# First attention of a two-block float32 model: projections and softmax steps in one stage, two heads a step

## The chip, the cores and the metric

The kernel runs on one core of a Trainium2 chip. The metric is the device time of one execution in microseconds; the median of several runs is compared. The engines are TensorE (PE, with its weight loads as PEld), VectorE (DVE), ScalarE (ACT), GpSimd (POOL) and SyncE (SP), which here only issues the weights' DMAs.

## The reference, cut to what matters

Two blocks of two layers run one after the other on 512 tokens of width 1024: attention, gated FFNs, a state-space layer, a convolution module, a differential attention, memory cross-attentions. The change touches only the first layer's attention: 8 heads over the whole past with a bias table (A), and 8 query heads on 2 key heads with a band of 128 past tokens and a sink (B).

```python
qa, ka, va, qb, kb, vb = jnp.split(h @ w_in, cuts, axis=-1)      # 18 blocks of 128 columns
qa, ka = rmsnorm(heads(qa, 8), q_norm_a), rmsnorm(heads(ka, 8), k_norm_a)     # over 64, per head
oa = band_attention(qa, ka, heads(va, 8), 8, relpos_table[:, idx], None)
qb, kb = rmsnorm(heads(qb, 8), q_norm_b), rmsnorm(heads(kb, 2), k_norm_b)
ob = band_attention(qb, kb, heads(vb, 2), 2, -slopes * abs(rel_b), sinks)
return concatenate([oa, ob], -1) @ w_out
# band_attention, per chunk of 64 queries:
sc = einsum(q, k) * 0.125 + bias                 # masked to the band
m = max(sc, sink); e = exp(sc - m)
p = e / (sum(e) + exp(sink - m));  out = p @ v
```

## The kernel before, in words

Every projection is a sum of three fp32r products: weights and activations are split into an upper and a lower part. SyncE loads slabs of 512 KB into 4 slots. ScalarE makes the upper part of a slab (`half`, L1840), GpSimd the lower one (`split_stream`, L503), three slabs ahead of TensorE. `gemm` (L545) runs 8 k-steps of three matmuls for each chunk of 128 output channels (L563 to L565) into one of four PSUM banks.

The first attention (`attn`, on TensorE L663, VectorE L1692, ScalarE L2210) has two phases with nothing interleaved.

The first computes 18 chunks: four of queries A, four of keys A, four of queries B, one of keys B, then five of values. VectorE multiplies a chunk by the row norm (L1710), ScalarE squares it (L2238), TensorE sums the squares over each head with a matmul by `head_ones` (L675), ScalarE takes the root (L2227), VectorE the reciprocal (L1717) and multiplies (L1720). Value chunks are transposed on TensorE (L588) and copied by ScalarE (L2221). All go to `qk` and `v_tok`.

The second (`attention`, TensorE L591, VectorE L1201, ScalarE L1867) works 64 units: one head and one tile of 128 queries each, heads A first (32 units with 128 to 512 keys), then heads B (32 units with 128 or 256 keys). Score, bias and mask are matmuls into one bank (L612): the table's bias is a F32 matmul of a reversing matrix `flip` with `rel`, the band's bias and the masks are bf16. VectorE takes the maximum (L1216) and negates it (L1218, or L1221 and L1223 with the sink). ScalarE takes the exponential with its row sum (L1886). VectorE takes the reciprocal (L1232) and scales the row of probabilities (L1235). TensorE transposes it (L625), three units later, ScalarE copies it (L1898), and TensorE multiplies with the values (L639), four units later: stationary 64 value columns, moving 128 queries, so the result comes out as channels by tokens, two heads in the halves of a bank. When a pair of heads is complete, ScalarE writes its upper part `oh` (L1905), VectorE the lower part `ol` (L1247). The output projection then reads them, chunk k behind `a_ol`.

The table is written to DRAM by ScalarE's queue (L2214) and read back in skewed rows by the same queue (`load_rel`, L2208). Each engine runs its instructions in the order written; semaphores hold it until the other engine has done its part.

The diff stage (`diff`, L702, L1267, L1920) near the end of the kernel works two maps of a head side by side (score L782) with projection k-steps between them (L720 to L722).

## Time and profile before

| | us |
|---|---|
| median of 3 runs | 3296.01 (3279.82 to 3302.17) |
| the profiled execution | 3287.4 |
| its span | 3285.5 |
| PE busy | 3129.9 (95%) |
| PEld busy | 2408.3 (73%) |
| DVE busy | 1550.0 (47%) |
| ACT busy | 1269.6 (39%) |
| POOL busy | 1178.6 (36%) |
| mean granted PE clock | 0.974 |

Busy time is the union of an engine's instructions; matmuls overlap, so a busy PE is not PE at its peak. The clock is a share of 2.4 GHz. A view of stretches gives, for each window of the span, the busy time of every engine with its instructions, the clock, the share of the DMA engines and GB/s. A timeline gives start, duration, engine, line, operation and tiles, and in brackets how long the engine was idle before and what ended it.

### The profile page before, as it was taken

What the parts mean: (1) busy time and instruction counts of PE and PEld (TensorE: products, weight loads), DVE (VectorE), ACT (ScalarE), POOL (GpSimd) and SP (SyncE); (2) the same over time, 40 slices, a digit from 0 to 9 for tenths busy, and PEclk for the clock granted to TensorE, in tenths of its full rate; (3) what the DMA queues carried; (4) which work ended last, traced back from release to release, by engine and by line L of the source; (5) the groups of instructions that cost most, each with busy time, mean ns of one, the idle gap of its engine ahead of it and who ended that gap; (6) DMA issues with size and microseconds to landing.
All of it is one profiled execution on the core that took longest, in us unless ns stands there. A gap on an engine that the chain in (4) does not pass through costs nothing.

```text
span 3285.5 us, 40113 instructions
## 1 busy us (share of the span) xinstructions
PE 3129.9 (95%) x13790; PEld 2408.3 (73%) x13790; DVE 1550.0 (47%) x2245; ACT 1269.6 (39%) x1974; POOL 1178.6 (36%) x495
## 2 busy tenths in 40 slices
PE   7999999998998899999998998999989999899998
PEld 5655888886675578888855777888867787788886
DVE  6445555327625744553268633332247763333322
ACT  3234444323334534443322433443233343344432
POOL 3300444443343034444432532444432254144443
PEclk9988999999999899999999999999999999999999
DMA  3200323332220022323311321332322132133332
GB/s 134 83 17 8 96 90 95 97 101 77 83 90 14 1 69 92 95 91 101 98 52 52 115 85 47 94 93 92 103 82 64 59 110 87 42 91 94 96 96 89
DMA packets 73290, 260.51 MB, mean 79 GB/s; under 512 B 8528, under 2 KB 8792, under 8 KB 72928
## 3 DMA queue, kind: packets, MB, share of 16 engines
q1 hardware_dynamic: 68400, 249.07, 24.7%
q10 hardware_dynamic: 4784, 10.05, 0.9%
q8 instruction: 64, 1.05, 0.1%
q14 instruction: 42, 0.34, 0.0%
HBM read 256.97 MB, written 2.12 MB: 79 GB/s over the span
## 4 chain that ended last, share of the span: by engine, by line
PE 43%; issue 36%; POOL 14%; DVE 5%; ACT 1%; POOLq 0%; ACTq 0%; DMA 0%; DVEq 0%
POOL w_lo L503 14%; PE bank L563 11%; PE bank L564 11%; PE bank L565 11%; PE bank L954 2%; DVE bank L1630 2%; PE bank L1081 1%; PE bank L1084 1%; PE bank L639 0%; PE bank L902 0%; PE bank L1098 0%; PE bank L904 0%; PE bank L903 0%; DVE c_u L1616 0%; PE bank L675 0%
## 5 line engine op out<-in xcount | busy, mean ns | idle before, releaser
L503 POOL TENSOR_TENSOR w_lo<-w_raw,w_hi 128x1024 fp32r<-128x1024 f32 x475 | 1145.9, 2414 | 1975.0 <-ACT w_hi L1840 1975.0
L563 PE MATMUL bank<-xh,w_hi 128*128 128x512 f32 x2008 | 811.1, 404 | 37.8 <-DVE xl L1153 15.1
L564 PE MATMUL bank<-xl,w_hi 128*128 128x512 f32 x2008 | 800.5, 399 | 0.0
L565 PE MATMUL bank<-xh,w_lo 128*128 128x512 f32 x2008 | 799.9, 398 | 0.0
L1840 ACT ACTIVATE w_hi<-w_raw 128x1024 fp32r<-128x1024 f32 x475 | 500.9, 1056 | 661.1 <-DMA w_raw<-w_glu_out 156.2
L563 PEld LDWEIGHTS bank<-xh,w_hi 128*128 128x128 f32 x2008 | 381.1, 190 | 145.3 <-issue 24.7
L564 PEld LDWEIGHTS bank<-xl,w_hi 128*128 128x128 f32 x2008 | 381.2, 190 | 95.0 <-issue 4.3
L565 PEld LDWEIGHTS bank<-xh,w_lo 128*128 128x128 f32 x2008 | 381.0, 190 | 93.1
L1186 DVE TENSOR_TENSOR xt<-bank,xt 128x512 f32 x72 | 49.8, 692 | 502.1 <-PE bank L565 502.1
L565 PE MATMUL bank<-hh,w_lo 128*128 128x512 f32 x704 | 279.1, 396 | 0.0
L563 PE MATMUL bank<-hh,w_hi 128*128 128x512 f32 x704 | 279.1, 396 | 0.0
L564 PE MATMUL bank<-hl,w_hi 128*128 128x512 f32 x704 | 279.1, 396 | 0.0
L1758 DVE TENSOR_TENSOR f_u<-bank,rstd 128x512 f32<-128x512 f32 x88 | 60.8, 691 | 275.4 <-PE bank L565 275.4
L1761 DVE TENSOR_TENSOR f_h<-f_y,f_u 128x512 f32<-128x512 f32 x88 | 154.0, 1750 | 7.2 <-ACT f_y L2264 0.3
L2269 ACT ACTIVATE hh<-f_h 128x512 f32 x88 | 55.6, 632 | 260.6 <-DVE f_h L1761 260.6
L564 PEld LDWEIGHTS bank<-hl,w_hi 128*128 128x128 f32 x704 | 132.6, 188 | 32.3
L563 PEld LDWEIGHTS bank<-hh,w_hi 128*128 128x128 f32 x704 | 132.6, 188 | 32.3
L565 PEld LDWEIGHTS bank<-hh,w_lo 128*128 128x128 f32 x704 | 132.6, 188 | 32.3
L1630 DVE SCALAR_TENSOR_TENSOR bank<-c_u,cols,bank 128x512 f32<-128x512 f32 x184 | 125.4, 747 | 44.1 <-PE bank L954 43.5
L1160 DVE TENSOR_TENSOR acc<-acc,sq 128x512 f32<-128x512 f32 x88 | 101.3, 1151 | 70.3 <-ACT sq L1831 70.3
L563 PE MATMUL bank<-oh,w_hi 128*128 128x512 f32 x320 | 128.0, 400 | 3.0 <-DVE ol L1680 2.4
L565 PE MATMUL bank<-oh,w_lo 128*128 128x512 f32 x320 | 126.8, 396 | 0.0
(309 smaller groups left out, 4410.7 us busy)
## 6 DMA issues: line engine op xcount, KB each, us to landing
w_raw<-w_ffn_in SPq DMA_DIRECT2D x88, 512.0 KB, 3.5
w_raw<-w_glu_in SPq DMA_DIRECT2D x88, 512.0 KB, 3.5
w_raw<-w_ffn_out SPq DMA_DIRECT2D x48, 512.0 KB, 3.5
w_raw<-w_glu_out SPq DMA_DIRECT2D x48, 512.0 KB, 3.5
w_raw<-w_ssm_in SPq DMA_DIRECT2D x41, 512.0 KB, 3.5
w_raw<-w_pw SPq DMA_DIRECT2D x24, 512.0 KB, 3.5
w_raw<-w_diff_in SPq DMA_DIRECT2D x24, 512.0 KB, 3.5
w_raw<-w_attn_in SPq DMA_DIRECT2D x18, 512.0 KB, 3.5
```

What stands on the lines that cost most here:

```text
L503: pool.tensor_tensor(w_lo[:, slot, :], w_raw[:, slot, :], w_hi[:, slot, :].bitcast(F32), ALU.subtract).then_inc(w_split, 1)
L563: pe.matmul(b, wh, hi[:, k, 0:n], start=(k == 0), stop=False)
L564: pe.matmul(b, wh, lo[:, k, 0:n], start=False, stop=False)
L565: mm = pe.matmul(b, wl, hi[:, k, 0:n], start=False, stop=last)
L954: mm = pe.matmul(conv_bank(p)[:], c_diag[:, p % 2, n, :], c_u[:, p % 3, n:n + S], start=(n == 0), stop=(n == CPE - 1))
L1160: dve.tensor_tensor(acc[:], acc[:], sq[:, j % 2, :], ALU.add).then_inc(x_acc, 1)
L1186: dve.tensor_tensor(row(xt, c), b[:], row(xt, c), ALU.add).then_inc(bank_free, 1)
L1630: ins = dve.scalar_tensor_tensor(conv_bank(p)[:], c_u[:, p % 3, k:k + S], col("dw_w", CONVW * p + k), conv_bank(p)[:], ALU.mult, ALU.add)
L1758: dve.tensor_tensor(f_u[:], bu[:], rstd[:], ALU.mult).then_inc(bank_free, 1)
L1761: dve.tensor_tensor(f_h[:], f_y[:], f_u[:], ALU.mult).then_inc(f_prod, 1)
L1840: act.activation(w_hi[:, slot, :], w_raw[:, slot, :], ACT.Copy).then_inc(w_half, 1)
L2269: act.activation(row(hh, p), f_h[:], ACT.Copy)\
```

## The change

The two phases become one loop of 32 steps (m), and a step is two heads and one tile of queries. The first four pairs are the banded heads B, the last four are heads A; the weight columns, norm gains, sinks and rows of the output weights are reordered for it. 34 k-steps of projections come first; then each step feeds three portions (x = 3m, 3m+1, 3m+2) of 1.5 k-steps on average, until all 144 are done. A chunk's eviction, its square, its sum over heads, root and reciprocal stand at fixed x (`attn_at`). Chunks use two banks, scores of a step two (four in turn), outputs and their transposes one, sums and value transposes one.

Both heads' scores are issued one behind the other, from partitions 0 to 63 and 64 to 127. The reversing matrix and the table are fp32r; the table is split in an upper and a lower part, two matmuls in place of one. Probabilities are not scaled; the transposed probabilities are now the stationary side and 64 value columns the moving one, so the result is tokens by channels; ScalarE scales it by the reciprocal of the sum while it copies it (`weighed`), and TensorE transposes the pair's 128x128 (`turn_out`). `oh` and `ol` are written per step. Square, sum and root use one buffer each, and root and reciprocal are taken in PSUM. Both table parts go to DRAM by ScalarE's queue and are read back by GpSimd's queue: the first two pairs' ahead of its split of slab 3, the rest behind the last slab of the input projection.

```diff
...
+        BM = 8 * NT
+        NB4 = 4 * NT
+        def is_rel(m):
+            return m >= NB4
+        def keys_of(m):
+            t = m % NT
+            if is_rel(m):
+                return 0, P * (t + 1)
+            return (0, P) if t == 0 else (P * (t - 1), 2 * P)
+        def attn_fed(x):
+            return min(18 * KD, 34 + 9 * (x + 1) // 6) if x >= 0 else 34
+        def attn_at(c, extra):
+            x = 0
+            while attn_fed(x) < min(KD * (c + 1) + extra, 18 * KD):
+                x += 1
+            return x + (1 if KD * (c + 1) + extra > 18 * KD else 0)
...
+        def step_bank(m, half):
+            return bank[2 + 2 * (m % 2) + half]
+        VALUES = (1, 8, 11, 14, 17)
+        NORMED = [c for c in range(18) if c not in VALUES]
...
+            def load_rel(pairs):
+                pool.wait_ge(rel_out, 32)
+                for pair in pairs:
+                    if pair >= 2:
+                        pool.wait_ge(b_score, 2 * (NB4 + NT * (pair - 1)))
+                    for h in (2 * pair, 2 * pair + 1):
+                        pool.dma_start(rel_h[:, h % 4, :], bass.AP(rel_dram_h, h * 767, [[1, P], [1, 640]]))\
+                            .then_inc(rel_buf[h % 4], 16)
+                        pool.dma_start(rel_l[:, h % 4, :], bass.AP(rel_dram_l, h * 767, [[1, P], [1, 640]]))\
+                            .then_inc(rel_buf[h % 4], 16)
...
+                def finish(c):
+                    if c:
+                        if c - 1 in VALUES:
+                            pe.wait_ge(v_ready, 2 + VALUES.index(c - 1) + 1)
+                        else:
+                            pe.wait_ge(q_ready, NORMED.index(c - 1) + 1)
+                    if c in VALUES:
+                        pe.wait_ge(bank_free, BANKS + st.chunk0 + c + 1)
+                        for t in range(NT):
+                            mm = pe.transpose(bank[7][:, t * P:(t + 1) * P], sq[:, 1, t * P:(t + 1) * P], ident[:])
+                        mm.then_inc(v_turned, 1)
                         return
-                    pe.wait_ge(q_sq, c + 1)
-                    if not isinstance(c, int) or c >= 2:
-                        pe.wait_ge(q_root, c - 1)
-                    pe.matmul(bank[5 + j % 2][:], head_ones[:], sq[:, j % 2, :], start=True, stop=True)\
-                        .then_inc(q_sum, 1)
-                def after(c, j):
-                    first_sum(c, j)
-                    if isinstance(c, int) and c == 0:
-                        pe.wait_ge(cst_ready, 4)
-                    lagged(fin, 17)(c, j)
-                gemm(st, xh, xl, S, x_ready(KD * nrm[0]), after, peel=4, tail=6)
-                keep_clock(8)
-                pe.wait_ge(q_ready, 13)
-                pe.wait_ge(flip_done, 2)
-                pe.wait_ge(v_ready, 2 + 5)
+                    pe.wait_ge(q_sq, NORMED.index(c) + 1)
+                    pe.matmul(bank[7][:], head_ones[:], sq[:, 0, :], start=True, stop=True).then_inc(q_sum, 1)
+                def score(m):
+                    pair, t = m // NT, m % NT
+                    k0, nk = keys_of(m)
+                    if t == 0:
+                        pe.wait_ge(q_ready, 5 + 2 * (pair - 3) if is_rel(m) else 2 + pair)
+                    if m >= 2:
+                        pe.wait_ge(b_copied, 2 * (m - 1))
+                    for half in range(2):
+                        lo, hi = 64 * half, 64 * half + 64
+                        q = b_q[lo:hi, (4 + pair - 4) % 6 if is_rel(m) else pair, t * P:(t + 1) * P]
+                        k = b_k[lo:hi, (pair - 4) % 3 if is_rel(m) else 3, k0:k0 + nk]
+                        pe.matmul(step_bank(m, half)[:, 0:nk], q, k, start=True, stop=False, skip_group_check=True)
+                    for half in range(2):
+                        b = step_bank(m, half)
+                        if is_rel(m):
+                            h = 2 * (pair - 4) + half
+                            if t == 0:
+                                pe.wait_ge(rel_buf[h % 4], 32 * (h // 4 + 1))
+                            first = 512 - P * t
+                            pe.matmul(b[:, 0:nk], flip_r[:], rel_h[:, h % 4, first:first + nk], start=False, stop=False,
+                                      skip_group_check=True)
+                            pe.matmul(b[:, 0:nk], flip_r[:], rel_l[:, h % 4, first:first + nk], start=False, stop=False,
+                                      skip_group_check=True)
+                            pe.matmul(b[:, nk - P:nk], ident_b[:], masks_b[:, 0, :], start=False, stop=True,
+                                      skip_group_check=True).then_inc(b_score, 1)
+                        else:
+                            pe.matmul(b[:, 0:nk], ident_b[:], alibi_b[:, 4 * half + pair, 256 - nk:256], start=False, stop=True,
+                                      skip_group_check=True).then_inc(b_score, 1)
...
+                def outputs(m):
+                    pair, t = m // NT, m % NT
+                    k0, nk = keys_of(m)
+                    if t == 0:
+                        pe.wait_ge(v_ready, 2 + 1 + max(pair - 3, 0))
+                    if m:
+                        pe.wait_ge(b_ol, m)
+                    vs = (pair - 4) % 3 if is_rel(m) else 3
+                    for half in range(2):
+                        u = 2 * m + half
+                        pe.wait_ge(b_copied, u + 1)
+                        o = 64 * half
+                        for kt in range(nk // P):
+                            v0 = k0 + kt * P + 64 * half
+                            mm = pe.matmul(bank[6][:, o:o + 64], b_pt[:, u % 4, kt * P:(kt + 1) * P], b_v[:, vs, v0:v0 + 64],
+                                           start=(kt == 0), stop=(kt == nk // P - 1), skip_group_check=True)
+                    mm.then_inc(b_pv, 1)
+                def turn_out(m):
+                    pe.wait_ge(b_otok, m + 1)
+                    pe.transpose(bank[6][:, P:2 * P], b_tok[:, m % 2, :], ident[:]).then_inc(b_ot, 1)
+                feed(KD)
+                norm_sum()
+                pe.wait_ge(cst_ready, 4)
+                feed(KD)
+                finish(0)
+                feed(KD)
+                finish(1)
+                feed(4)
+                finish(2)
+                feed(6)
...
+                for m in range(BM + 2):
+                    if m < BM:
+                        score(m)
+                    for f in range(3):
+                        x = 3 * m + f
+                        feed(attn_fed(x) - attn_fed(x - 1))
+                        for c in range(3, 18):
+                            if attn_at(c, 3) == x:
+                                finish(c)
+                        if f == 0 and 2 <= m <= BM + 1:
+                            outputs(m - 2)
+                        if f == 1 and 1 <= m <= BM:
+                            turn(m - 1)
+                        if f == 1 and 2 <= m <= BM + 1:
+                            turn_out(m - 2)
                 vt[0] = 5
-                attention(*UNITS["attn"])
-                gemm(ST["attn_out"], oh, ol, S, lambda k: pe.wait_ge(a_ol, k + 1))
+                pe.wait_ge(bank_free, BANKS + wo.chunk0)
+                gemm(wo, oh, ol, S, lambda k: pe.wait_ge(b_ol, NT * (k + 1)))
             vt, au, at, ag = [0], [0], [0], [0]
...
-                    dve.wait_ge(q_rec, c + 1)
-                    dst = row(qk, c)
-                    dve.scalar_tensor_tensor(dst, dst, col("g_qk", c),
-                                             rt, ALU.mult, ALU.mult).then_inc(q_ready, 1)
...
+                def peak(m):
+                    _, nk = keys_of(m)
+                    cs = slice(2 * m, 2 * m + 2)
+                    for half in range(2):
+                        u = 2 * m + half
+                        dve.wait_ge(b_score, u + 1)
+                        top = dve.reduce_max(b_stat[:, 0, u:u + 1], step_bank(m, half)[:, 0:nk], AX_X)
+                        if half:
+                            step(top)
+                    if is_rel(m):
+                        dve.tensor_scalar(b_stat[:, 1, cs], b_stat[:, 0, cs], -0.125, None, ALU.mult).then_inc(b_max, 1)
+                        return
+                    sink = sink_c[:, 2 * (m // NT):2 * (m // NT) + 2]
+                    step(dve.scalar_tensor_tensor(b_stat[:, 0, cs], b_stat[:, 0, cs], 0.125, sink, ALU.mult, ALU.max))
+                    step(dve.tensor_scalar(b_stat[:, 1, cs], b_stat[:, 0, cs], -1.0, None, ALU.mult))
+                    dve.tensor_tensor(b_stat[:, 5, cs], sink, b_stat[:, 1, cs], ALU.add).then_inc(b_max, 1)
+                def weigh(m):
+                    cs = slice(2 * m, 2 * m + 2)
+                    dve.wait_ge(b_exp, 2 * m + 2)
+                    if not is_rel(m):
+                        dve.wait_ge(b_sink, m + 1)
+                        step(dve.tensor_tensor(b_stat[:, 2, cs], b_stat[:, 2, cs], b_stat[:, 3, cs], ALU.add))
+                    dve.reciprocal(b_stat[:, 4, cs], b_stat[:, 2, cs]).then_inc(b_rec, 1)
+                def low(m):
+                    ch, t = m // NT, m % NT
+                    dve.wait_ge(b_oh, m + 1)
+                    dve.tensor_tensor(ol[:, ch, t * P:(t + 1) * P], bank[6][:, P:2 * P],
+                                      oh[:, ch, t * P:(t + 1) * P].bitcast(F32), ALU.subtract).then_inc(b_ol, 1)
...
+                for m in range(BM + 2):
+                    if m < BM:
+                        peak(m)
+                    for f in range(3):
+                        x = 3 * m + f
+                        for c in range(3, 18):
+                            if attn_at(c, 3) == x - 1:
+                                finish(c)
+                        for c in range(4, 18):
+                            if attn_at(c, 0) == x:
+                                evict(c)
+                        if f == 0 and 1 <= m <= BM:
+                            weigh(m - 1)
+                    if 2 <= m <= BM + 1:
+                        low(m - 2)
                 vt[0] += 5
-                dve.wait_ge(q_ready, 13)
-                attention(*UNITS["attn"])
                 residual(ST["attn_out"], new_x(nxt[s]))
...
+                def powers(m):
+                    _, nk = keys_of(m)
+                    act.wait_ge(b_max, m + 1)
+                    for half in range(2):
+                        u = 2 * m + half
+                        if m >= 2:
+                            act.wait_ge(b_turn, u - 3)
+                        act.activation(b_prob[:, u % 4, 0:nk], step_bank(m, half)[:, 0:nk], ACT.Exp,
+                                       bias=b_stat[:, 1, u:u + 1], scale=0.125, accum_out=b_stat[:, 2, u:u + 1])\
+                            .then_inc(b_exp, 1)
+                    if not is_rel(m):
+                        cs = slice(2 * m, 2 * m + 2)
+                        act.activation(b_stat[:, 3, cs], b_stat[:, 5, cs], ACT.Exp).then_inc(b_sink, 1)
+                def copied(m):
+                    _, nk = keys_of(m)
+                    for half in range(2):
+                        u = 2 * m + half
+                        act.wait_ge(b_turn, u + 1)
+                        if m >= 2:
+                            act.wait_ge(b_pv, m - 1)
+                        act.activation(b_pt[:, u % 4, 0:nk], step_bank(m, half)[:, 0:nk], ACT.Copy).then_inc(b_copied, 1)
...
+                def weighed(m):
+                    act.wait_ge(b_pv, m + 1)
+                    act.wait_ge(b_rec, m + 1)
+                    if m >= 2:
+                        act.wait_ge(b_ot, m - 1)
+                    for half in range(2):
+                        u, o = 2 * m + half, 64 * half
+                        cp = act.activation(b_tok[:, m % 2, 64 * half:64 * half + 64], bank[6][:, o:o + 64], ACT.Copy,
+                                            scale=b_stat[:, 4, u:u + 1])
+                    cp.then_inc(b_otok, 1)
...
+                for m in range(BM + 2):
+                    if m < BM:
+                        powers(m)
+                    for f in range(3):
+                        x = 3 * m + f
+                        for c in range(3, 18):
+                            if attn_at(c, 3) == x:
+                                finish(c)
+                        for c in range(4, 18):
+                            if attn_at(c, 0) == x:
+                                square(c)
+                        while turned[0] < 18 + LEAD and attn_fed(x) >= min(KD * (turned[0] - LEAD) + 6, 18 * KD):
+                            next_slab()
+                        if f == 0 and 2 <= m <= BM + 1:
+                            weighed(m - 2)
+                        if f == 1 and 1 <= m <= BM:
+                            copied(m - 1)
+                    if 2 <= m <= BM + 1:
+                        upper(m - 2)
                 vt[0] += 5
-                act.wait_ge(rel_out, 16)
-                act.wait_ge(sink_in, 16)
-                for h in range(4):
-                    load_rel(h, None)
-                attention(*UNITS["attn"])
...
```

## Rows read from the trace of the kernel before

**Rows 1.** Busy time in stretches: window, length, engines (instructions), PEclk, DMA share, GB/s
```profile
13.00:154.00 141.00, 126.88 (x487) 93.85 (x488) 85.32 (x66) 47.22 (x65) 46.01 (x20) 0.95 0.26 86
154.00:245.00 91.00, 87.11 (x374) 48.46 (x372) 36.02 (x128) 31.27 (x95) 2.22 (x1) 0.87 0.11 33
245.00:317.00 72.00, 66.23 (x301) 38.33 (x300) 45.97 (x201) 36.62 (x140) 0.00 (x0) 0.81 0.00 1
294.00:310.00 16.00, 16.00 (x51) 8.74 (x50) 8.16 (x34) 6.09 (x24) 0.00 (x0) 0.50 0.00 0
2460.00:2670.00 210.00, 209.87 (x1163) 157.92 (x1163) 161.22 (x364) 83.57 (x201) 65.79 (x27) 1.00 0.21 66
```

**Rows 2.** Timeline of PE: the first matmul of the output projection
```profile
315.62 0.50 PE L563 MATMUL bank<-oh,w_hi 128*128 128x512 f32 x1
```

**Rows 3.** Timeline of PE in the projections: sum over heads, two neighbouring matmuls
```profile
38.02 1.02 PE L675 MATMUL bank<-sq,head_ones 128*128 128x512 f32 x2
...
44.02 0.40 PE L564 MATMUL bank<-xl,w_hi 128*128 128x512 f32 x1
44.26 0.39 PE L565 MATMUL bank<-xh,w_lo 128*128 128x512 f32 x1
```

**Rows 4.** Timeline of PE, table units, 512 keys, from one head to the next
```profile
231.86 1.12 PE L612 MATMUL bank<-qk 64*128 64x512 f32 x2
232.92 1.12 PE L612 MATMUL bank<-rel,flip 128*128 128x512 f32 x2
...
233.94 0.28 PE L625 MATMUL bank<-ident,a_prob_t 128*128 128x128 f32 x1
234.14 1.09 PE L639 MATMUL bank<-a_pt_t,v_tok 128*64 128x128 f32 x8
235.16 0.48 PE L612 MATMUL bank<-qk 64*128 64x128 f32 x2
...
241.85 1.12 PE L612 MATMUL bank<-qk 64*128 64x512 f32 x2
```

**Rows 5.** Timeline of PE, fp32r matmuls of 256 columns
```profile
1795.80 0.28 PE L902 MATMUL bank<-m_hi,w_hi 128*128 128x256 f32 x1
1795.92 0.28 PE L903 MATMUL bank<-m_lo,w_hi 128*128 128x256 f32 x1
```

**Rows 6.** Timeline of PE in diff, scores of two maps side by side
```profile
2585.97 1.13 PE L782 MATMUL bank<-d_k,d_q 64*128 64x512 f32 x4
```

**Rows 7.** Timeline of all engines, one banded unit: maximum, sink, exponential
```profile
284.57 0.41 DVE L1216 TENSOR_REDUCE a_stat<-bank 128x1 f32<-128x256 f32 x1
...
285.46 0.29 ACT L1885 ACTIVATE a_stat<-sink_c,a_stat 128x1 f32<-128x1 f32 x1 [1.53 <-DVE a_stat L1223]
...
285.66 0.46 ACT L1886 ACTIVATE a_prob_t<-bank,a_stat 128x256 f32<-128x256 f32 x1
```

**Rows 8.** Groups by line, 0 to 420 us: count, busy us, mean ns, idle before
```profile
L1717 DVE RECIPROCAL a_prob_t<-a_prob_t 128x512 f32<-128x512 f32 x13 | 43.6, 3351 | 8.2 <-ACT a_prob_t L2227 8.2
...
L1720 DVE SCALAR_TENSOR_TENSOR qk<-qk,cols,a_prob_t 128x512 f32 (+1 forms) x13 | 9.8, 751 | 1.4 <-DVE a_prob_t L1717 1.2
```

**Rows 9.** Timeline of ACT in the state scan: table loads around a root
```profile
1064.68 1.28 ACT L2117 ACT_TABLE_LOAD   x1
...
1066.68 1.28 ACT L2092 ACT_TABLE_LOAD   x1
```

**Rows 10.** A line's durations (min/median/max ns) in diff; a split's group (page)
```profile
L1350 DVE TENSOR_TENSOR d_q<-d_q,acc x8: 691/2742/2744, 2459.4 to 2640.1; 128x512 f32<-128x512 f32 x8
...
L503 POOL TENSOR_TENSOR w_lo<-w_raw,w_hi 128x1024 fp32r<-128x1024 f32 x475 | 1145.9, 2414 | 1975.0 <-ACT w_hi L1840 1975.0
```

**Rows 11.** Timeline of DVE: the first projection chunk leaves PSUM
```profile
33.85 0.69 DVE L1710 TENSOR_TENSOR qk<-bank,rstd 128x512 f32<-128x512 f32 x1
```

**Rows 12.** The line that reads the table: issue ns, landing us (min/median/max)
```profile
L2208 ACTq DMA_DIRECT2D rel<-rel_table x8: 326/334/654, 153.3 to 205.1; - x8
...
DMA to landing us min/median/max: 3.1/4.4/6.3
```

## What the change does to the time: the prediction

> **What bounds the kernel now.** Over the span TensorE is nearly always busy, so a saving must come out of its own time or out of stretches in which it waits. I cut the first attention out of the trace with the view of busy time in stretches [rows 1]. It has three parts with three limits. From 13 to 154 us the 18 projection chunks run; VectorE is busy 85 us of 141 and ScalarE 47, beside TensorE. From 154 to 245 us run the 32 units with a position table, TensorE busy 87 of 91 us. From 245 to 317 us run the 32 banded units; each is small, and TensorE waits in turn for VectorE and ScalarE. The granted clock is 0.81 there, and 0.50 (1.2 GHz) from 294 to 310 us, where the row still calls TensorE fully busy. The output projection begins at 315.62 us [rows 2]; that is the mark which the change can move. The last row of [rows 1] is the attention near the end of the kernel (function diff): 32 steps of two heads with projection matmuls fed between them, 210 us, TensorE busy 209.87, clock 1.00. The change gives that shape to the first attention, so it is my yardstick.
>
> **Prices on TensorE.** At full clock projection matmuls start 0.24 us apart (44.02, 44.26; over a chunk 0.234), and a sum over a head's square, two instructions in F32, takes 1.02 us with its latency, 0.92 in the stream [rows 3]. A table unit at t=3 takes [rows 4]: scores 1.06 us (231.86 to 232.92), table bias in F32 with the bf16 mask 1.02, one transpose 0.20, four outputs 1.02 and thus 0.25 each with the wait. The F32R matmul of 256 columns starts every 0.12 us [rows 5]. Two heads side by side in diff take 1.13 us for four score instructions of 512 columns [rows 6], no more than one head's two: they run together, in two halves of the array.
>
> **The change, part by part.**
> - *Scores.* Per step of two heads 0.42, 0.63, 0.84, 1.05 us for 128 to 512 keys, what one head takes now.
> - *Bias.* Four F32R matmuls a step in place of two F32, 0.10 to 0.234 each, with two masks 0.6, 0.7, 0.9, 1.15 us. Banded steps keep bf16, 0.25.
> - *Transposes*: 0.11 each and 0.1 for a wait: 0.42 to 1.08 a step, banded 0.64. They take unweighted probabilities; the scaling of whole rows leaves VectorE and comes back on ScalarE over 64 columns.
> - *Output by query.* The moving side halves to 64 columns, the stationary side doubles to 128. No row has an F32 pair of this shape. Bounds: half of the 0.21 now, or all of it. I take 0.20, as the weights are now the longer of the two; 136 of them, so the lower bound gives 14 us more. With waits 0.68 to 1.88 a step, banded 1.08. One transpose of the result is added, 0.20.
> - *Sum.* Table steps t=0 to 3: 2.3+3.25+4.25+5.35=15.2 us, 3.8 a step; banded 2.0+3x2.8=10.4, 2.6 a step. Now: two heads of four table units take 20 us (9.99 each, 231.86 to 241.85), 5.0 a step, and banded 72/16=4.5.
> - *Feeding.* 1.5 k-steps three times a step, 4.5x3x0.234=3.16 us. 34 of 144 k-steps come before step 0, so 24.4 of the 32 steps are fed: all 16 banded and 8.4 table steps.
>
> **The ring.** In step m TensorE issues score(m), two feeds, outputs(m-2), turn(m-1), then turn_out(m-2), which waits for weighed(m-2). On ScalarE that is queued behind powers(m), and so behind peak(m) on VectorE. Banded [rows 7]: two maxima of 0.42 and three small steps of some 0.2 with their hand-overs, 1.6 us; two exponentials of 0.46 and 0.2 for the sink, 1.1; weighed 0.45; crossings 0.3: 3.5 us, against 2.1+1.08+0.64=3.8 of TensorE work. It just fits. A chunk's normalisation doesn't: a reciprocal of 3.35 and a product of 0.75 us [rows 8], 11 times inside the loop, every 1.78 steps. Where it stands in the first two thirds of step m, the reciprocal follows the root, peak(m+1) is queued behind it, powers(m+1) behind that, and TensorE halts at turn_out(m-1): followed through, 15.1 us for two steps instead of 12.9, so 2.2 lost. Three such in banded steps 6.6; three in the last third 0.5 each; the first 2; slab copies ahead of weighed 3: stalls 13. In fed table steps TensorE has more work of its own, and I take 3.
>
> The root lies between exponentials, so two table loads come with each. In the state scan a load of 1.28 us stands before the root and one behind it [rows 9], back to back with their neighbours. The one before is in my 2.2; the one behind runs while ScalarE waits for the next peak, its cover; uncovered, the 11 cost 14 us. The Trainium skill ("ScalarE: Activation LUTs", What ACT_TABLE_LOAD costs and Table sets) speaks against such an order: it wants functions batched by set, and puts a switch at 2.66 us with its drain. By it the 22 loads would be an estimated 58 us of ScalarE; the rows, without a drain, make it 28.
>
> *Port.* VectorE's sum of two SBUF tensors took 2.74 us, 0.69 at its shortest, in diff, where GpSimd's splits of 2.41 run beside it [rows 10]. Banded steps have three small ones of the kind, and GpSimd now runs there. Nothing to 2 us for each of 10 splits; I take 3 us in all.
>
> *Start.* The first projection leaves PSUM at 34.5 [rows 11]; a square, a slab copy and an issue later, 36.6, the table goes to DRAM, and lands at 39.7 by the shortest landing of [rows 12]. GpSimd then issues eight DMAs ahead of its split of slab 3, which the fourth chunk wants at 45. No row has a DMA issued by GpSimd. Bounds: ScalarE's 0.33 us an issue [rows 12], with which nothing waits, and GpSimd's own longest work, 2.41, with which the split ends at 61, 16 us late. I take 1.0, nearer to the like operation: 39.7+8+2.4=50, 5 late. The second group's scores lie steps ahead. After the remaining ten k-steps, a sum and a reciprocal score(0) stands at 59.
>
> **The sum.** Start 59. Banded 16x(2.6+3.16)=92.2, seven sums 6.4, values 1.2, stalls 13, port 3: 116. Fed table steps 8.4x6.96=58.5, sums and values 4.9, stalls 3: 66. The 7.6 steps without feed leave the ring uncovered: score, maxima, exponentials, weighing and copies make 4.4, 4.3, 5.4, 6.9 for t=0 to 3, mean 5.3: 40. From the last unit to the output projection, 4 beyond its ring. Clock in that tail, 4. Together 289. My prices applied to diff (six k-steps 4.2, scores 0.74, masks, transposes and outputs 1.25, rotations and sums 0.8) give 7.0 us a step where it took 210/32=6.5 [rows 1]; over the fed steps that is 12 us too much, of which I take a third off, since less TensorE work uncovers the ring: 285. Against 315.6, 30 us less. The profiled execution (3287.4) would take 3257, and the median of the runs, 3296, 3266.
>
> **Rivals.**
> - *TensorE never waits*, as in diff: no stalls (16), none in the tail (7.6x1.5=11), none at the start or for the clock (8): 250, 66 us saved, 3230. For it: 209.87 busy of 210. Against: diff has no reciprocal, and its score waits for exponentials alone. 0.20.
> - *The ring turns serially*, the other side. If root with both loads, square, slab copy, eviction and reciprocal all fall on the path, a chunk adds 4.9+4.8=9.7 us in 1.78 steps, 5.4 a step, to 5.1: 10.5x24.4=256, with 59+40+8 it makes 363, 47 us more than now: 3343. It decides from 8.5 us a fed step on, where the saving is gone. 0.07.
> - *The clock falls* to 1.2 GHz in the tail and part of the banded steps, as at 294 us. Twenty us of TensorE work at half speed cost 20: 3286. For it: the tail is 70% filled. Against: the feeds. 0.13.
> - *GpSimd's DMAs are dear*: 11 us more, 3277. 0.08.
> - *Side by side does not run together* here: 0.74x32=24 us more, 3290. Against: [rows 6]. 0.04.
> - *My forecast*: 0.48.
>
> **How the numbers follow.** Under 1%, 33 us, can't be told from no change here. Faster by more: the first rival and half of my own case, 0.44. Slower by more: the serial ring, 0.07. Within 1%: 0.49. The range goes from the first rival to past the clock and side-by-side cases, 3230 to 3302.
>
> **What would show it.** The first output-projection matmul near 285 us; score(m) 5.3 to 6.5 us apart in fed banded steps, about 7 in fed table steps, 5.3 after step 24, with longer gaps where a root stands in the first two thirds; some 22 more table loads; a gap with eight DMA issues on GpSimd before its fourth split. I am wrong if TensorE's waits at the transposed output are longer than 2.5 us each, if VectorE's small two-input sums take 2 us each time, or if the granted clock is below 0.9 between 60 and 250 us.

## The result and the profile after

The changed kernel takes 3263.42 us, the median of 9 runs (3259.1 to 3270.06), where the kernel before takes 3296.01 (3279.82 to 3302.17): a ratio of 0.9916, with a 95% interval of 0.9897 to 0.9934. That is 33 us less, just on the border that the prediction drew between "faster" and "within 1%". The forecast was 3266. The profiled execution has a span of 3260.4 us against 3285.5, 25.1 less.

The mark that the change can move is the first matmul of the output projection. Timeline of TensorE in the kernel changed:

```profile
290.05 0.76 PE L610 MATMUL bank<-oh,w_hi 128*128 128x512 f32 x1
```

It stood at 315.62 [rows 2], so it comes 25.6 us earlier. The span is 25.1 shorter: what is gained stays, and nothing behind the first attention moved. The view of busy time in stretches, cut where scores start (step 0, step 16, step 24, step 31, output projection), answers to [rows 1]:

```profile
58.30:173.72 115.42, 97.64 (x497) 68.70 (x497) 62.84 (x148) 71.06 (x193) 21.09 (x9) 0.96 0.13 41
173.72:234.06 60.34, 56.91 (x314) 41.02 (x313) 27.60 (x51) 37.60 (x92) 13.48 (x13) 1.00 0.27 81
234.06:272.16 38.10, 30.87 (x195) 22.05 (x194) 12.37 (x38) 19.00 (x66) 2.94 (x2) 0.91 0.05 16
272.16:290.05 17.89, 15.53 (x63) 12.33 (x64) 2.57 (x8) 5.30 (x17) 0.00 (x0) 0.54 0.00 0
```

The columns are the window, its length, the busy time of TensorE, its weight loads, VectorE, ScalarE and GpSimd, the granted clock, and the DMA share. The 16 banded steps leave TensorE idle for 17.8 of 115.4 us, the eight fed table steps for 3.4 of 60.3. In the last row it is called busy for 15.5 of 17.9 us, at a clock of 0.54, so near 1.2 GHz.

What TensorE waited for between 13 and 300 us (total us, times, longest), from the view of waits; the lines left out at the head (20.1 us) lie before 30 us and stand alike in the kernel before (19.7):

```profile
...
PE bank L816 <- ACT b_tok L2471: 12.8, 14, 1.7
PE bank L810 <- DVE ol L1910: 7.9, 7, 2.2
PE bank L767 <- DVE b_q L1880: 5.7, 1, 5.7
...
PE bank L767 <- ACT b_pt L2462: 3.7, 9, 0.8
PE bank L810 <- issue: 3.3, 2, 2.3
```

L816 is turn_out, L810 the outputs, L767 the scores, L753 the sum over a chunk's square. The wait at the turned output is the one that the prediction named; its longest is 1.7 us. The wait at the outputs is one that the prediction had no term for: outputs(m-2) waits until VectorE has taken the lower part of the step before out of bank 6, and that subtraction stands behind whatever reciprocal VectorE is at. The third line is score(0), which waits for the first queries (chunk 2).

Nearly half of the 12.8 us at turn_out (6.0) lies behind 234 us, where no chunk is left. The 16 banded steps alone, 58.3 to 173.72 us (the line left out is score(0)'s 5.7, which ends where the window begins):

```profile
PE bank L810 <- DVE ol L1910: 5.8, 4, 2.2
...
PE bank L816 <- ACT b_tok L2471: 4.6, 5, 1.7
PE bank L753 <- ACT sq L2428: 2.9, 1, 2.9
PE bank L810 <- issue: 2.3, 1, 2.3
PE bank L767 <- ACT b_pt L2462: 2.1, 4, 0.8
```

These five lines make up all but 0.1 of the 17.8 us in which TensorE stands idle there. The outputs have 8.1 of them, turn_out 4.6. One of the waits at the outputs, the 2.17 us that end at 147.84, as VectorE and ScalarE show it:

```profile
140.78 3.36 DVE L1877 RECIPROCAL bank<-bank 128x512 f32<-128x512 f32 x1
...
145.96 0.67 DVE L1870 TENSOR_TENSOR b_k<-bank,rstd 128x512 f32<-128x512 f32 x1
147.50 0.29 DVE L1910 TENSOR_TENSOR ol<-bank,oh 128x128 fp32r<-128x128 f32 x1 [0.86 <-ACT oh L2478]
```

```profile
146.67 0.63 ACT L2428 ACTIVATE sq<-b_k 128x512 f32<-128x512 f32 x1 [2.76 <-DVE b_k L1870]
```

The eviction stands behind the reciprocal, its square holds ScalarE's copy of the upper part, and the lower part waits for that copy. Two of the five waits at the outputs (3.6 us) come this way; in the other three (4.6 us) the subtraction follows directly on the reciprocal and its product.

The groups of VectorE and ScalarE that answer to [rows 8, 9]:

```profile
L1877 DVE RECIPROCAL bank<-bank 128x512 f32<-128x512 f32 x11 | 37.0, 3364 | 24.0 <-ACT bank L2439 24.0
...
L1904 DVE TENSOR_TENSOR b_stat<-b_stat 128x2 f32<-128x2 f32 x16 | 4.8, 303 | 0.0
```

```profile
L2448 ACT ACT_TABLE_LOAD x12 | 15.4, 1283 | 1.2 <-DVE b_stat L1897 1.0
...
L2439 ACT ACT_TABLE_LOAD x11 | 14.1, 1283 | 0.2
```

The reciprocal costs the same as before (3364 ns against 3351), and 11 of the 13 are now inside the loop. There are 23 table loads, 1.28 us each.

### The profile page after: what moved, and what is told of

It reads as the page before. It is cut to its first block, busy times and chain, and to the rows that moved or that the text cites. A ratio compares the mean times of both kernels' runs of the same rounds, so it can differ in the third digit from the quotient of the medians.

```text
span 3260.4 us, 40032 instructions
## 1 busy us (share of the span) xinstructions
PE 3083.4 (95%) x13814; PEld 2393.4 (73%) x13814; DVE 1521.9 (47%) x2127; ACT 1307.6 (40%) x2069; POOL 1186.2 (36%) x511
## 4 chain that ended last, share of the span: by engine, by line
PE 43%; issue 33%; POOL 14%; DVE 7%; ACT 2%; POOLq 0%; DMA 0%; ACTq 0%; DVEq 0%; SPq 0%
POOL w_lo L547 14%; PE bank L610 11%; PE bank L612 11%; PE bank L611 11%; PE bank L1109 2%; DVE bank L1785 2%; DVE bank L1877 1%; PE bank L1236 1%; PE bank L1239 1%; PE bank L1057 1%; PE bank L1058 0%; PE bank L1059 0%; PE bank L686 0%; PE bank L726 0%; PE bank L1253 0%
## 5 line engine op out<-in xcount | busy, mean ns | idle before, releaser
L610 PE MATMUL bank<-xh,w_hi 128*128 128x512 f32 x1864 | 745.3, 400 | 18.9 <-POOL w_lo L547 14.2
L611 PE MATMUL bank<-xl,w_hi 128*128 128x512 f32 x1864 | 740.0, 397 | 0.0
L612 PE MATMUL bank<-xh,w_lo 128*128 128x512 f32 x1864 | 739.8, 397 | 0.0
L610 PEld LDWEIGHTS bank<-xh,w_hi 128*128 128x128 f32 x1864 | 351.7, 189 | 114.9 <-POOL w_lo L547 21.6
L611 PEld LDWEIGHTS bank<-xl,w_hi 128*128 128x128 f32 x1864 | 351.8, 189 | 86.1 <-issue 1.7
L612 PEld LDWEIGHTS bank<-xh,w_lo 128*128 128x128 f32 x1864 | 351.8, 189 | 85.8
L611 PE MATMUL bank<-ol,w_hi 128*128 128x512 f32 x320 | 128.2, 401 | 0.0
```

The lines of the kernel that those rows point to most:

```text
L610: pe.matmul(b, wh, hi[:, k, 0:n], start=(k == 0), stop=False)
L611: pe.matmul(b, wh, lo[:, k, 0:n], start=False, stop=False)
L612: mm = pe.matmul(b, wl, hi[:, k, 0:n], start=False, stop=last)
```

## Experiments

Each kernel is the changed one with one edit, or two where said. "Mark" is the first matmul of the output projection (290.05 in the kernel changed). One profiled execution tells the mark to about 4 us only: steps 12 and 13, the same code in both, took 17.7 us in the kernel changed and 21.8 in the one with dummy matmuls from step 26 on, the granted clock in them being 1.00 and 0.73. So stretches are compared where the clock is alike, and the medians beside them. The span of the kernel changed is 3260.4, its median 3263.42. The experiments ran in three groups, in which the kernel before had medians of 3286.69 (reciprocals, table loads, two heads, normalisation), 3289.0 (table later, bias, dummies, slower feed) and 3290.41 (the last four) in place of 3296.01; medians are compared within a group, ratios across groups. The kernel with the table read later (3262.25) is all but the kernel changed and serves as its stand-in in the second.

### The reciprocals

```
-    dve.reciprocal(bank[7][:], bank[7][:]).then_inc(q_rec, 1)
+    w = 512 if c < 3 else 1
+    dve.reciprocal(bank[7][:, 0:w], bank[7][:, 0:w]).then_inc(q_rec, 1)
```

> The changed kernel with one thing left out: in the loop (chunks 3 and on) VectorE's reciprocal of the sum is taken of one column instead of 512, so the queries and keys are not normalised rightly. It takes 11 x 3.2 us off VectorE and nothing off TensorE or ScalarE. Theory (the reciprocal keeps the next maximum, the next eviction and the lower part waiting, and TensorE behind them): the loop up to the first matmul of the output projection, 58.3 to 290.05 us in the changed kernel, gets 11 to 17 us shorter. Rival 1 (the root and its two table loads on ScalarE are what is in the way): 0 to 4 us. Rival 2 (TensorE's own work sets the steps, as in diff): nothing.

Measured: 3249.87 us (3244.07 to 3251.83), ratio to the kernel before 0.9889 [0.9855, 0.9923], span 3242.3, mark 268.28. Cut at the same steps as above:

```profile
56.63:156.84 100.21, 94.94 (x497) 68.06 (x497) 40.70 (x148) 70.96 (x193) 21.05 (x9) 0.97 0.16 47
156.84:214.88 58.04, 56.65 (x313) 41.12 (x312) 18.19 (x52) 37.64 (x92) 13.47 (x13) 1.00 0.29 84
214.88:251.28 36.40, 29.32 (x195) 21.17 (x194) 11.77 (x36) 18.71 (x66) 2.94 (x2) 0.95 0.05 16
251.28:268.28 17.00, 13.17 (x64) 10.65 (x64) 2.47 (x8) 5.30 (x17) 0.00 (x0) 0.68 0.00 0
```

From step 0 to the mark it takes 211.65 us against 231.75, 20.1 less, more than the theory's 11 to 17. Of that 15.2 lie in the banded steps and 2.3 in the next eight; the 2.6 behind step 24 come with a higher clock (0.87 against 0.79). The span is 18.1 us shorter, but this profile is the fastest of four runs: the ratio is lower by 0.27%, some 9 us, and the intervals overlap. In the same group the kernel without table loads has a median of 3259.2, 9.3 above this one, and no run of the one falls among those of the other; so the sign is clear, and the size is some 9 to 18 us of the whole. In the banded steps TensorE's idle time falls from 17.8 to 5.3 us, and in the next eight from 3.4 to 1.4, so the reciprocals cause about two thirds of the stalls in the fed steps. What is left in the banded steps:

```profile
...
PE bank L816 <- ACT b_tok L2472: 3.4, 5, 0.9
PE bank L767 <- ACT b_pt L2463: 1.2, 3, 0.5
PE bank L810 <- DVE ol L1911: 0.6, 1, 0.6
```

Of the 12.5 us that go, 7.5 were at the outputs, 2.9 at the sum, 0.9 at the scores and only 1.2 at turn_out.

### The table loads

```
-    act.activation(bank[7][:], bank[7][:], ACT.Sqrt, scale=1.0 / 64, bias=eps[:, 0:1]).then_inc(q_root, 1)
+    if c < 3:
+        act.activation(bank[7][:], bank[7][:], ACT.Sqrt, scale=1.0 / 64, bias=eps[:, 0:1]).then_inc(q_root, 1)
+    else:
+        act.activation(bank[7][:], bank[7][:], ACT.Copy, scale=1.0 / 64).then_inc(q_root, 1)
```

> The changed kernel with one thing left out: in the loop ScalarE's root is replaced by a scaled copy of the same tile, so 22 table loads of 1.28 us fall away (12 + 11 rows at these two lines in the changed kernel, one each remains) and the normalisation is wrong. Theory (one load of the two in the path, in two thirds of the cases): 3 to 8 us shorter. Rival (each switch in full, by the rule of the Trainium skill, ScalarE: Activation LUTs, Table sets): 25 us or more.

Measured: 3259.2 us (3253.93 to 3261.23), ratio 0.9915 [0.9887, 0.9942], span 3259.4, mark 289.27. With the 22 loads and their 28 us of ScalarE gone, the mark gains 0.8 us and the ratio nothing. But the stretches say more. Steps 0 to 11, in the kernel changed and here, at the same clock:

```profile
58.30:144.22 85.92, 74.01 (x367) 51.68 (x367) 48.18 (x108) 55.28 (x144) 15.04 (x7) 0.94 0.11 37
```

```profile
57.09:137.62 80.53, 73.49 (x366) 51.53 (x366) 48.53 (x108) 39.22 (x132) 15.09 (x7) 0.94 0.13 40
```

This is 5.4 us less, and TensorE is idle for 7.0 in place of 11.9; the two later kernels that change nothing before step 12 (bias in one part, dummies) took 85.2 and 85.8. The eight fed table steps took 59.1 against 60.3. Steps 12 and 13 took 20.1 at a clock of 0.85 (17.7 at 1.00 in the kernel changed), and from step 24 to the mark it took 60.2 against 56.0, the clock being 0.74 against 0.79; there 4.3 us of the gain go. So in the fed steps the loads cost about 6 us, within the theory's 3 to 8, and most of their 28 us is hidden while ScalarE waits for VectorE. That the whole kernel gains from their absence is not shown; whether the lower clock behind them came by chance stays open.

### Two heads not side by side

```
-                    for half in range(2):
                         b = step_bank(m, half)
```

(The loop that issued both scores and then both biases becomes one loop over the heads: score, bias, score, bias.)

> Nothing left out: the matmuls of a step in another order, scores and bias of the first head, then those of the second, so no two score matmuls on the two halves of the array stand next to each other. Theory (side by side they run together): each step's scores cost 0.42 to 1.05 us more on TensorE, 24 us in all; of that 12 to 22 us appear at the output projection, since some falls into waits. Rival (the halves do not run together in this order of banks either way): within 2 us.

Measured: 3289.74 us (3284.27 to 3292.66), ratio 1.0015 [0.9998, 1.0031], span 3282.5, mark 314.48, 24.4 later, where 12 to 22 was expected. Without this part of the change the kernel is as slow as before. In the fed steps it costs 8.6 us (3.3 in the banded ones, 5.3 in the first eight table steps); the rest, 16.3 us, falls behind step 24, where the granted clock was 0.63 on the mean against 0.79 and the same matmuls last longer (step 0 stands 0.5 us earlier). How much of the 16.3 is matmul time and how much clock is not separated. Ten runs bear out the size: the ratio is 1.0% higher, some 33 us.

### The table read later

GpSimd's eight DMA issues are moved four slabs back, from ahead of its split of slab 3 to ahead of that of slab 7 (the loop behind starts a turn later):

```
+    late = st.name == "attn_in"
+    if late:
+        turn(0, 4)
+        turn(1, 4, first)
-    if first is not None:
+    elif first is not None:
...
```

> Nothing left out: GpSimd reads the first two pairs' tables back four slabs later, ahead of its split of slab 7 instead of slab 3; they are wanted at step 16 only. Theory (their 2.6 MB share the DMA engines with slabs 5 and 6, ScalarE waits 3.6 and 6.5 us for slabs to land, and the root of chunk 2 is queued behind that): score(0) starts at 53 to 55 us instead of 58.3, and the output projection 3 to 5 us earlier. Rival (the eight issues of 0.58 us on GpSimd, which hold the split of slab 3, are what is late): the same gain, but ScalarE's waits for slabs stay at about 10 us in all. Rival 2 (the start is bound by sum, root and reciprocal of chunk 2): less than 1.5 us.

Measured: 3262.25 us (3258.88 to 3264.4), ratio 0.9913 [0.9884, 0.9942], span 3261.4, mark 289.86. ScalarE's waits for slabs, in the timelines of the kernel changed and of this one:

```profile
43.01 1.06 ACT L2049 ACTIVATE w_hi<-w_raw 128x1024 fp32r<-128x1024 f32 x1 [3.59 <-DMA w_raw<-w_attn_in]
...
52.46 1.06 ACT L2049 ACTIVATE w_hi<-w_raw 128x1024 fp32r<-128x1024 f32 x1 [6.54 <-DMA w_raw<-w_attn_in]
```

```profile
44.06 1.06 ACT L2053 ACTIVATE w_hi<-w_raw 128x1024 fp32r<-128x1024 f32 x1 [2.02 <-DMA w_raw<-w_attn_in]
...
50.64 1.06 ACT L2053 ACTIVATE w_hi<-w_raw 128x1024 fp32r<-128x1024 f32 x1 [2.09 <-DMA w_raw<-w_attn_in]
```

So the table's transfers delayed the weight slabs: both waits together fall from 10.1 to 4.1 us, where the rival, the issues on GpSimd, would have left them at 10. Score(0) starts 1.8 us earlier (56.49), less than the theory's 3 to 5; but this profile stood 2.1 us behind already at the first square on ScalarE (36.75 against 34.66), ahead of anything that the edit moves. From that square to score(0) it took 19.7 us here, 23.6 in the kernel changed, and 22.0 to 23.3 in the other kernels that leave the table in its place. So the transfers cost 2 to 4 us there. Score(12) comes 2.9 us earlier and score(28) still 2.2. What is left at the mark is 0.2: between steps 28 and 29 the gain goes, where this profile's clock was 0.50 between 250 and 260 us.

### The bias in one F32 part

```
-    pe.matmul(b[:, 0:nk], flip_r[:], rel_h[...], ...)
-    pe.matmul(b[:, 0:nk], flip_r[:], rel_l[...], ...)
+    pe.matmul(b[:, 0:nk], flip[:], rel_h[...], ...)
...
```

(`rel_h` and its copy in DRAM become plain F32.)

> The table's bias as one F32 matmul in place of two fp32r ones (the table's lower part is read in but not added, so the bias is a little less exact; its DMAs stay). Theory, by the prices of the kernel before (0.33 to 0.97 us for F32 against twice 0.10 to 0.234): TensorE's work in the 16 table steps grows by 10 us; 6 to 10 us later at the output projection. Rival (the table steps have slack enough): under 3 us.

Measured: 3268.9 us (3265.98 to 3272.99), ratio 0.9941 [0.992, 0.9963], span 3267.6, mark 293.98. The mark is 3.9 us later where 6 to 10 was expected, and not all of it is the bias: 2.2 us lie in the banded steps, which the edit doesn't touch (steps 12 and 13 ran at 0.84 here). The eight fed table steps take 62.9 against 60.3, so 2.5 us there. Behind step 24 it takes the same (56.2 against 56.0), but at a clock of 0.90 against 0.79, so the bias costs there too, by an amount that these profiles don't give. Against the kernel with the table read later the median is 6.7 us higher, and no run of the one falls among those of the other, so a cost is shown; of its size only that it may be the 6 to 10 expected.

### Dummy matmuls in the tail

```
+    if m == 26:
+        pe.wait_ge(v_ready, 2 + 5)
+    if m >= 26:
+        keep_clock(4)
     turn_out(m - 2)
```

> Nothing left out: four matmuls of zeros and masks (bf16, 384 columns, 0.65 us together) that nobody reads are added ahead of each wait for the transposed output from step 26 on, where no projection is fed any more. Theory (the last steps and the way out run at 1.2 GHz because TensorE stands idle 1.5 us a step): the granted clock from 272 us to the output projection is above 0.9 instead of 0.54, and the output projection starts 3 to 6 us earlier. Rival (the ring of the three engines sets this stretch, at either clock): 0 to 4 us later.

Measured: 3256.7 us (3252.96 to 3260.31), ratio 0.9896 [0.9867, 0.9926], span 3256.7, mark 286.00. Cut at steps 24 and 31:

```profile
237.16:272.51 35.35, 30.94 (x214) 22.34 (x213) 12.33 (x38) 18.89 (x66) 2.93 (x2) 1.00 0.04 16
272.51:286.00 13.49, 11.12 (x75) 7.96 (x76) 2.47 (x8) 5.26 (x18) 0.00 (x0) 1.00 0.00 1
```

From step 24 to the mark there are 289 recorded matmuls instead of 258; the clock stays at 1.00, and from step 24 to the mark it takes 48.8 us against 56.0. The low clock thus costs at least 7.2 us of the kernel changed, 4.4 of them behind step 31. (Before step 24 this profile was 3 us behind, so the mark shows 4.) Against the kernel with the table read later the median is 5.5 us lower, though some runs of the two overlap.

### A slower feed

```
-    return min(18 * KD, 34 + 9 * (x + 1) // 6) if x >= 0 else 34
+    return min(18 * KD, 34 + 9 * (x + 1) // 7) if x >= 0 else 34
```

> Nothing left out: 9 k-steps in 7 portions instead of 9 in 6, so that the projections last to step 28 instead of 24. Theory (the waits of the steps without feed are covered, 4 x 1.5 us, while the banded steps lose a little to the ring because they have less TensorE work): 1 to 6 us earlier at the output projection. Rival (in the banded steps the ring is what counts and each keeps its length): 3 to 10 us later.

Measured: 3269.9 us (3260.34 to 3270.16), ratio 0.9926 [0.9902, 0.9951], span 3268.1, mark 293.33. The mark is 3.3 us later where 1 to 6 less was expected, and the median is 7.7 above that of the kernel with the table read later. But 3 us is within what one profile can be off, and the five runs spread over 9.8 us and overlap those of the other. So the expected gain is not there; a loss is likely, and not shown. The clock in steps 0 to 11 was 0.85 here against 0.94, with 340 recorded matmuls in them instead of 367.

### The normalisation behind the maxima

```
-    if attn_at(c, 3) == x - 1:
+    if f == 0 and attn_at(c, 3) // 3 == m - 1:
         finish(c)
```

> Nothing left out: VectorE takes a chunk's reciprocal and product always right behind the maxima of the next step, never ahead of them. Same instructions, another place in VectorE's order. Theory (what costs is that peak(m+1) is queued behind the reciprocal, 2.2 us at each of six places): 5 to 12 us shorter to the output projection. Rival (what costs is VectorE's time as such, or the lower part and the evictions that come late behind it): no gain, or slower by up to 5.

Measured: 3276.64 us (3274.08 to 3282.31), ratio 0.9963 [0.9947, 0.9979], span 3272.3, mark 300.14: 10 us later, where 5 to 12 less was expected. ScalarE's waits between 60 and 272 us, in this kernel and in the kernel changed:

```profile
ACT sq L2428 <- DVE b_k L1870: 11.4, 4, 3.6
ACT sq L2428 <- DVE b_q L1870: 7.2, 3, 3.5
```

```profile
ACT sq L2428 <- DVE b_q L1870: 3.6, 2, 2.7
ACT sq L2428 <- DVE b_k L1870: 3.5, 2, 2.8
```

And step 17 of this kernel, VectorE, ScalarE and TensorE:

```profile
184.29 3.35 DVE L1877 RECIPROCAL bank<-bank 128x512 f32<-128x512 f32 x1
187.68 0.75 DVE L1880 SCALAR_TENSOR_TENSOR b_q<-b_q,cols,bank 128x512 f32<-128x512 f32 x1
188.34 0.68 DVE L1870 TENSOR_TENSOR b_k<-bank,rstd 128x512 f32<-128x512 f32 x1
...
189.06 0.63 ACT L2428 ACTIVATE sq<-b_k 128x512 f32<-128x512 f32 x1 [3.63 <-DVE b_k L1870]
189.59 0.50 ACT L2471 ACTIVATE b_tok<-bank,b_stat 128x64 f32<-128x64 f32 x2
```

The maxima do go first here. But the eviction of the next chunk stands behind the reciprocal, its square waits for it on ScalarE, and the weighing of the output is queued behind the square; TensorE waited 4.1 us at turn_out for it. Of the 10 us 7.4 lie in the eight fed table steps, 4.7 of them in step 17 alone. So the place of the reciprocal matters by what it does to the eviction too, and here that outweighs what the maxima gain.

### Outputs by channel

```
-    pe.matmul(bank[6][:, o:o + 64], b_pt[:, u % 4, kt * P:(kt + 1) * P], b_v[:, vs, v0:v0 + 64], ...)
+    pe.matmul(bank[6][o:o + 64, 0:P], b_v[:, vs, v0:v0 + 64], b_pt[:, u % 4, kt * P:(kt + 1) * P], ...)
```

> One part of the change undone alone: the outputs again take 128 queries as the moving side and a head's 64 value columns as the stationary one, 136 of them, all else as it is (a head's output then stands by value channel where the rest takes it by query, so the attention's output is wrong; the work is otherwise whole). Theory: the prediction's price, 0.20 us an output by query against 0.21 to 0.25 by channel; the kernel changed shows 1.00 us for eight instructions, 0.25 an output, waits and latency in it. So the two shapes cost alike: output projection within 3 us of 290.05, span 3257 to 3264. Rival: an output costs by its moving columns, 0.11 against 0.21, and by channel is 136 x 0.10 = 14 us dearer, span 3270 to 3275 (a part hidden in the waits at the turned output, so from 3268). A third: two heads by channel stand in two halves of the array and run together, 136 x 0.1 less, span 3246 to 3252.

Measured: 3255.6 us (3251.72 to 3259.93), ratio 0.9899 [0.9859, 0.994], span 3252.5, mark 286.35. Step 19, four outputs and the feed behind them, in the kernel changed and in this one:

```profile
197.66 0.39 PE L728 MATMUL bank<-xh,w_lo 128*128 128x512 f32 x1
197.89 1.00 PE L810 MATMUL bank<-b_v,b_pt 128*128 128x64 f32 x8
198.69 0.47 PE L726 MATMUL bank<-xh,w_hi 128*128 128x512 f32 x1
```

```profile
197.92 0.40 PE L728 MATMUL bank<-xh,w_lo 128*128 128x512 f32 x1
198.25 0.66 PE L810 MATMUL bank<-b_pt,b_v 128*64 128x128 f32 x8
198.84 0.50 PE L726 MATMUL bank<-xh,w_hi 128*128 128x512 f32 x1
```

By query, four outputs hold the stream for 0.80 us (197.89 to 198.69), 0.20 each: the price taken. By channel the two heads' outputs overlap, and from one feed matmul to the next it is 0.92 us against 1.03, so some 0.03 less an output, 4 us over 136. That is the third expectation in kind, at a third of its size. The 24 steps from step 0 on took 176.1 us against 175.8, no gain; without steps 12 and 13, where the clock was 0.86 here and 1.00 there, they took 1.8 less. The other 3.6 us come behind step 24, where the clock was also higher (0.78 against 0.54 behind step 31). So the shape matters little to the fed steps, and how much of the rest is shape and how much clock stays open. The intervals of the ratios overlap.

### Logarithm and exponential in place of root and reciprocal

```
-    act.activation(bank[7][:], bank[7][:], ACT.Sqrt, scale=1.0 / 64, bias=eps[:, 0:1]).then_inc(q_root, 1)
+    act.activation(bank[7][:], bank[7][:], ACT.Ln, scale=1.0 / 64, bias=eps[:, 0:1]).then_inc(q_root, 1)
+    act.wait_ge(q_root, NORMED.index(c) + 1)
+    act.activation(bank[7][:], bank[7][:], ACT.Exp, scale=-0.5).then_inc(q_rec, 1)
...
-    dve.wait_ge(q_root, n + 1)
-    dve.reciprocal(bank[7][:], bank[7][:]).then_inc(q_rec, 1)
```

> The thirteen roots on ScalarE and reciprocals on VectorE (L2439, L1877) become two activations on ScalarE: the logarithm of the mean square, then the exponential of minus half of it. The whole output is computed. Theory, from the run without the reciprocal (20 us of attention) and the one without the table loads (about 1): VectorE loses 13 x 3.36 us of work and ScalarE gains 13 x 0.65; output projection at 269 to 274 against 290.05, span 3241 to 3248. Rival 1: the ring's holder is now ScalarE, whose chain is longer by an activation a chunk and keeps its table loads or gets a third one, so that 11 x (0.65 + 0.3 + 1.28) = 25 us eat the gain up: span 3256 to 3268. Rival 2: half of it is eaten: 3249 to 3255.

Measured: 3268.96 us (3262.9 to 3272.75), ratio 0.9941 [0.9921, 0.996], span 3266.2, mark 292.33 where 269 to 274 was expected: the first rival, by its span. ScalarE's timeline:

```profile
95.73 1.28 ACT L2437 ACT_TABLE_LOAD   x1
97.02 0.66 ACT L2437 ACTIVATE bank<-bank,eps 128x512 f32<-128x512 f32 x1
97.70 1.28 ACT L2439 ACT_TABLE_LOAD   x1
99.00 0.58 ACT L2439 ACTIVATE bank<-bank 128x512 f32<-128x512 f32 x1
99.49 0.44 ACT L2462 ACTIVATE b_pt<-bank 128x128 f32<-128x128 f32 x2
```

There are still two loads a chunk, one ahead of the logarithm and one ahead of the exponential; and the second now stands between the two activations, so ScalarE is held for 3.76 us (95.73 to 99.49) with the copy of the turned probabilities queued behind. TensorE's waits for that copy grow from 3.7 us to 9.2 and those at the turned output from 12.8 to 16.6, while those at the outputs shrink from 11.2 to 5.5. In the banded steps it is idle for 14.6 us and in the next eight for 7.0, where it was 5.3 and 1.4 without the reciprocals; in the banded steps 11.5 of the 14.6 are waits for ScalarE, against 9.6 of 17.8 in the kernel changed. Of the 3.76 us the loads are 2.57; how much of the lost gain is theirs, and how much the added activation's, no run separates. The Trainium skill ("ScalarE: Activation LUTs", Table sets) names a set that holds both functions and would need one load; no run here shows it.

### The same with the dummies, and with the slower feed

> The kernel before this one, and with it the dummy matmuls of the warm tail (four small ones a step from step 26 on). The whole output is computed. Theory: the two gains lie in different places, 20 us in the fed steps and 4 in the tail, and add up: output projection at 265 to 270, span 3236 to 3244, granted clock 1.00 between the last step and the output projection. Rival: without the reciprocal the tail is fuller and keeps its clock, the dummies are only in the way: span as in the run before or 1 to 2 us more.

Measured: 3254.14 us (3252.37 to 3256.11), ratio 0.9895 [0.9856, 0.9934], span 3251.1, mark 283.39, the clock 1.00 from step 31 on. This is 8.9 us at the mark from the dummies, twice their gain alone, and 14.8 of the median. The mark is far from the expected 265 to 270, since the logarithm had not brought the 20 us that the sum counted on. The banded steps (112.4 us) are 3 us shorter than in the kernel changed, the next eight 5 longer. Its median is the lowest of the kernels that compute everything, but its ratio can't be told from that of the kernel changed (0.9916 [0.9897, 0.9934]).

> The same two changes, and the feeding of projection matmuls stretched from 24.4 steps to 28.5 (dummies from step 29 on). The whole output is computed. Theory of the ring: an unfed step lasts 5.3 us by its ring alone while TensorE has about 3.8 us of work in it, so a fed step wastes nothing and an unfed one 1.5; four more fed steps gain 4 x 1.5 = 6 us against the run before, span 3230 to 3238. The slower feed alone lost 3 us (output projection 293.33 against 290.05), which this theory puts down to the reciprocals falling on worse places. Rival: what it lost by is the later keys and queries themselves, which the scores wait for at the head changes, whatever the reciprocal: 3 to 8 us slower than the run before, span 3240 to 3250.

Measured: 3259.29 us (3257.95 to 3264.62), ratio 0.9912 [0.9882, 0.9942], span 3256.3, mark 286.09, 2.7 us later than the run before. The median is 5.2 higher, and no run of the one falls among those of the other, so here the slower feed does lose. One step shows where: step 27, which is still fed here and unfed in the other kernel, took 12.2 us (6.2 there) with a wait of 2.9 at turn_out, as a normalisation falls into it: logarithm, exponential and their loads hold ScalarE from 250.08 to 253.84, and the weighing is queued behind them. So the later feed carries the chunk work of ScalarE and VectorE into steps whose ring is longest (512 keys). The theory had put the loss of the slower feed on the reciprocals; there is a loss with them gone, so that was wrong, though two activations with two loads now stand in their place.

## Why the prediction was right

Its sum was nearly right before the last correction: 59 + 116 + 66 + 40 + 4 + 4 = 289 against a mark of 290.05. That the scores of two heads run together was right, and it carries most of the gain; the stalls came out right in size, but largely by another path than the one forecast. Point by point:

- **Start.** 59 forecast, 58.3 measured, partly for other reasons. GpSimd issued its DMAs in 0.54 to 0.72 us each, not 1.0, from 37.5 to 41.9 us, and TensorE waited for no split behind them. What was late was a slab, 6.5 us of wait on ScalarE with the table's transfers beside it, and the root of the first queries is queued behind that slab's copy; its reciprocal and product then end the 5.7 us that score(0) waited. The run with the table read later shows this: 2.0 and 2.1 us of wait, and 2 to 4 us less to score(0).
- **Banded fed steps.** 116 forecast, 115.4 measured. The work of TensorE was put at 99.8 us and is 95 to 98; the stalls and the port at 16, and it is idle for 17.8. Without the reciprocals 5.3 are left. So the reciprocals are the main cause, as forecast, but the path was wrong, and the agreement of the size is in good part luck. The prediction followed the reciprocal through the maxima and the exponentials to turn_out, 2.2 us at each of three places. Only 4.6 of the 17.8 us are at turn_out, and 3.4 of these stay without the reciprocals. The wait that it had no term for, at the outputs, has 8.1 us and loses 7.5: the lower part stands behind the reciprocal, directly or by way of eviction, square and upper part. The path through maxima and exponentials does show once, but it ends at the sum of a square (2.9 us at 71.96), not at turn_out. The run with the normalisation behind the maxima put that path right and lost 10 us, 4.7 of them in the one step where the eviction's path is seen.
- **The table loads.** One of two was put in the path, some 3 to 8 us. The mark of the run without them shows 0.8, but its steps 0 to 11 are 5.4 us shorter at the same clock and the fed table steps 1.2, so in the fed steps the price was about right. The Trainium skill ("ScalarE: Activation LUTs", What ACT_TABLE_LOAD costs) puts a switch at 2.66 us with its drain; here each load shows 1.28 us and the next activation starts directly behind it. By its price the 22 loads were an estimated 58 us of ScalarE, by the rows 28, and about 6 show in the fed steps: the rest is covered by ScalarE's waits for VectorE.
- **Fed table steps.** 7.54 us each, against 66/8.4=7.9 forecast: over the 8.4 steps 3 us less.
- **The port.** The small sums of L1904 took 303 ns on the mean, 149 at their shortest, so 16 x 0.154 = 2.5 us more than at their shortest; 3 were taken. That the splits on GpSimd cause it was not tested. They don't take 2 us each, which would have made the forecast wrong.
- **Unfed steps.** Steps 25 to 30 took 31.9 us, 5.3 each, as forecast. Part of this is luck: the forecast had no low clock in them, and with the clock held they took 29.1, 4.9 each, dummies and all.
- **From step 31 to the mark.** This is the term that was mis-sized. Its ring of 6.9 us, 4 beyond it and 4 for the clock made 14.9; it took 17.9. With the clock held at 1.00 it took 13.5, dummies and all, so 2.6 too little stood for the work and 0.4 for the clock there. But the clock costs 2.8 us more in the seven steps before it, which had no term.
- **The third of 12.** The prices applied to diff gave 7.0 us a step where it took 6.5, and 4 us were taken off for it. That was the wrong step: the prices fitted the fed steps here without it, and the mark would have been forecast 1 us from where it stands. That 1 us is itself a balance: in the sum the tail was some 5 us too short and the other parts some 4 too long. With the 4 us taken off, 285 was 5 too early.
- **Side by side.** 24 us were set on it; taking it away moved the mark by 24.4, and the ratio by some 33 us. Of this 8.6 lie in the fed steps, the rest came with a lower clock, so the agreement is partly luck.
- **Bias in two parts.** Its prices give some 10 us of TensorE's work; 2.5 show in the fed table steps and 6.7 in the medians, and the mark's 3.9 is in part the clock of steps that have no table. The price is neither shown nor refuted.
- **The median.** The mark is 25.6 us earlier and the span 25.1 shorter, while the medians differ by 32.6 and the ratio by 22 to 34 us. The forecast took 30 off 3296, 5 more than the mark and the span moved. It comes so close to 3263 because 3296.01 was a high median of the kernel before: in its other three groups of runs (42 in all) it had 3286.69 to 3290.41, 23 to 27 us above 3263.42. That is luck.

Of the rivals, TensorE that never waits fell by the 33 us of waits in the list and by 17.8 us of idle time in the banded steps; the serial ring by 7.2 us a fed step against 8.5. The low clock kept to the tail (0.54 behind step 31, 0.96 in the banded steps) and cost at least 7 us, not 20. GpSimd's issues were cheap, 0.54 to 0.72 us each, though their transfers were not.

## What to carry to other kernels

When projections are fed into an attention loop, follow a long VectorE instruction through every queue behind it: here the subtraction that frees the output bank, and the eviction with its square on ScalarE, weighed more than the maxima that looked critical. What a table load costs depends on its place: 22 loads, 28 us of ScalarE, cost about 6 us of the fed steps where ScalarE mostly waited anyhow. Before a long unfed tail is accepted, look at the clock it will run at; some dummy matmuls in its waits were worth 4 to 9 us at the mark here. And before a single profile's total is read, compare stretches at the same clock: at the mark the loads seem to cost nothing, since stretches behind the fed steps, at a lower clock, took back what their absence had gained.

## What the hardware showed that was not expected

- Four outputs with 128 stationary and 64 moving columns in F32 hold TensorE for 0.80 us; the same four with 64 stationary and 128 moving columns, two heads in two halves of the array, for about 0.1 less. Halving the moving side gained nothing that shows.
- The tail of the attention ran at a granted clock of 0.54 though TensorE counted as busy for 15.5 of 17.9 us; with 75 matmuls behind step 31 instead of 63, and 214 instead of 195 in the seven steps before, it stayed at 1.00.
- GpSimd issues a DMA in 0.54 to 0.72 us, against 0.33 on ScalarE [rows 12]. With eight such transfers beside it a slab was waited for 6.5 us (4.0 to 7.0 in the twelve kernels that have them there), with them behind it 2.1.
- The sum of two SBUF tensors of 2 columns took 0.15 us at its shortest, 0.30 on the mean and once 1.01, where another small step (L1895) took 0.19 on the mean.
